# Four output buffers, other homes and places for some weight blocks, in a one-core encoder layer

## The reference

```python
proj = x @ w_in[i]
aq, ak, av, ag, bq, bk, bv, bg = jnp.split(proj, split_at, axis=-1)
ya = chunk_relbias_attention(aq, ak, av, rel_bias[i]) * jax.nn.silu(ag)
yb = sliding_window_sink_gqa(rope(bq), rope(bk), bv, sinks[i]) * jax.nn.silu(bg)
mix = jnp.concatenate([ya, yb], axis=-1) @ w_out[i]
h = DN_ALPHA * x + mix
h = h + jax.nn.sigmoid(h @ w_ple_gate[i]) * (p[i] @ w_ple_proj[i])
x = layer_norm(h, ln_g[i], ln_b[i])
```

## Time and profile before

| | us |
|---|---|
| median of 3 runs (2604.04 to 2610.0) | 2608.16 |
| the profiled execution, its own time | 2606.84 |
| its span, first to last instruction | 2605.1 |
| TensorE busy | 2480.7 (95%) |
| TensorE weight load busy | 2161.2 (83%) |
| VectorE busy | 1695.0 (65%) |
| ScalarE busy | 1193.5 (46%) |
| GpSimd busy | 379.3 (15%) |

### The profile page before, as it was taken

How to read it: one execution, slowest core, us unless ns; L and a number is a source line. 1 busy time by engine, 2 the same in 40 slices (tenths; PEclk the granted TensorE clock), 3 DMA queues, 4 the chain that set the end, 5 groups by cost and what they waited for, 6 DMA issues and landing times. The chain is left out here.

```text
span 2605.1 us, 37929 instructions
## 1 busy us (share of the span) xinstructions
PE 2480.7 (95%) x13620; PEld 2161.2 (83%) x13620; DVE 1695.0 (65%) x3215; ACT 1193.5 (46%) x2438; POOL 379.3 (15%) x226
## 2 busy tenths in 40 slices
PE   6999999999999999989999999968999999999997
PEld 4778887888789778989999998966888888888886
DVE  7887788768886888378888886863424333333333
ACT  4343443343333434278888887962222222222322
POOL 0100000000000000000000000123343434444341
PEclk9999999999999999999999998989999999999998
DMA  3645265435544554565666547965544545354540
GB/s 133 199 151 157 105 207 161 140 124 192 165 121 157 183 158 108 185 211 184 210 209 195 179 128 250 317 181 159 114 120 112 121 110 123 108 127 113 126 113 24
DMA packets 352693, 402.52 MB, mean 155 GB/s; under 512 B 83856, under 2 KB 257056, under 8 KB 346784
## 3 DMA queue, kind: packets, MB, share of 16 engines
q1 hardware_dynamic: 348544, 390.34, 50.8%
q0 software_dynamic: 4000, 10.25, 1.2%
HBM read 265.50 MB, written 136.07 MB: 154 GB/s over the span
## 5 line engine op out<-in xcount | busy, mean ns | idle before, releaser
L1638 DVE TENSOR_TENSOR y_lo<-y_raw,y_hi 128x1024 fp32r<-128x1024 f32 x32 | 39.2, 1226 | 396.2 <-ACT y_hi L1138 396.2
L980 ACT ACTIVATE wop_hi<-w_raw 128x512 fp32r<-128x512 f32 x288 | 174.1, 622 | 179.1 <-DVE w_raw L1279 153.6
L925 POOL DMA_DIRECT2D yb_d<-y_b x32 | 20.4, 637 | 1616.8 <-ACT y_b L1180 1591.0
L1538 DVE CUSTOM_DVE_ANT_0 prob<-psum,bias 128x640 f32<-128x640 f32 (+4 forms) x256 | 199.3, 778 | 73.6 <-issue 73.0
L1109 ACT ACTIVATE prob<-prob,small 128x640 f32<-128x640 f32 (+4 forms) x256 | 203.9, 797 | 60.7 <-DVE small L1538 60.7
L1740 PE MATMUL psum<-xs_lo_b,wop_hi 128*128 128x512 f32 x528 | 207.9, 394 | 0.0
L1740 PE MATMUL psum<-xt_hi,wop_hi 128*128 128x512 f32 x480 | 190.0, 396 | 16.7 <-issue 7.2
L1740 PE MATMUL psum<-wo_hi,y_hi 128*128 128x512 f32 x512 | 202.8, 396 | 1.3 <-DVE wo_lo L1633 1.3
L1554 DVE TENSOR_TENSOR pt_lo<-psum,pt_hi 128x640 fp32r<-128x640 f32 (+4 forms) x256 | 199.2, 778 | 4.2 <-ACT pt_hi L1118 4.2
L1740 PE MATMUL psum<-wo_hi,y_lo 128*128 128x512 f32 x512 | 200.2, 391 | 0.0
L1740 PE MATMUL psum<-wo_lo,y_hi 128*128 128x512 f32 x512 | 200.1, 391 | 0.0
(11 more groups left out here) (210 smaller groups left out, 6465.6 us busy)
## 6 DMA issues: line engine op xcount, KB each, us to landing
w_raw<-in_w_blocks SPq DMA_DIRECT2D x168, 256.0 KB, 3.9
qk_d<-stage_out SPq DMA_DIRECT2D x72, 512.0 KB, 4.1
v_d<-stage_out SPq DMA_DIRECT2D x64, 320.0 KB, 2.4
bq_d<-stage_out SPq DMA_DIRECT2D x64, 256.0 KB, 4.0
g_d<-stage_out SPq DMA_DIRECT2D x64, 256.0 KB, 2.3
ya_d<-y_a SPq DMA_DIRECT2D x128, 128.0 KB, 2.5
bq<-bq_d SPq DMA_DIRECT2D x32, 512.0 KB, 5.8
y_two<-ya_d SPq DMA_DIRECT2D x32, 512.0 KB, 4.6
```

Of the source, the lines that this page charges most:

```text
L925: pool.dma_start(yb_d[pair * P:pair * P + 4 * HEAD, t0:t0 + 4 * CHUNK].rearrange("(h d) t -> d h t", d=HEAD), y_b[:, d % 2, :, :]).then_in ...
L980: act.activation(wop_hi[:, n % W_RING, :, :], w_raw[:, i, :, :], ACT.Copy).then_inc(w_hi_done, 1)
L1538: dve.tensor_tensor_reduce(out=prob[:, r, NBW - n * P:NBW].rearrange("p (a b) -> p a b", a=2), in0=psum[:, 0:2, 0:n * P // 2], in1=bias[:, ...
L1638: dve.tensor_tensor(y_lo[:, :, :], y_raw[:, s, :, :], y_hi[:, :, :].bitcast(f32), ALU.subtract).then_inc(y_split, 1)
```

## The change

The product stage: A22 of the pairs 2, 4, 6 and 8 is loaded to a part of `x_raw_b`, that of the others to place 6 of `w_raw` as before (`a22(a)`), and from pair 2 on the load is issued with the other three blocks of its pair, at product (a-2, 6). At a group's change VectorE splits ring block 4 ahead of the low part of X22, and block 5 between it and the sums of T4. The attention of group B: `y_b` takes 128 partitions in place of 64, which gives four buffers, with four semaphores; a copy waits for the store of d-4. The passage: y tile 0 is split after strip 3 (step 67) in place of before strip 0 (step 64), on both engines; the reciprocals are copied before y tile 1 is split; w_ple's two strips get places of their own (`wp_raw`, over `wp_lo`) and are loaded right after strip 15. The matmuls, their order and the arithmetic are the same.

Context lines are left out of the diff.

```diff
@@ -58,8 +58,8 @@
-STRIP_SLOT = (0, 1, 2, 3, 4, 5, 11, 12, 3, 4, 5, 6, 7, 8, 9, 10, 6, 7)
-STRIPS = 13
+STRIP_SLOT = (0, 1, 2, 3, 4, 5, 11, 12, 3, 4, 5, 6, 7, 8, 9, 10, 13, 14)
+STRIPS = 15
@@ -285,6 +285,9 @@
+        def a22(a):
+            return x_raw_b[:, 1, 0, :].rearrange("p (k m) -> p k m", m=P) if a in (2, 4, 6, 8) else w_raw[:, 6, :, :]
+
@@ -315,7 +318,7 @@
-        y_b = sb("y_b", [HEAD, 2, 4, 4 * CHUNK])
+        y_b = sb("y_b", [P, 2, 4, 4 * CHUNK])
@@ -323,7 +326,9 @@
-        wp_hi, wp_lo = (sb(n, [P, 2, D_MODEL], f32r) for n in ("wp_hi", "wp_lo"))
+        wp_hi = sb("wp_hi", [P, 2, D_MODEL], f32r)
+        wp_raw = under("wp_raw", [P, 2, D_MODEL])
+        wp_lo = sb("wp_lo", [P, 2, D_MODEL], f32r)
@@ -351,7 +356,9 @@
-            return h[slot - 10][:, :]
+            if slot < 13:
+                return h[slot - 10][:, :]
+            return wp_raw[:, slot - 13, :]
@@ -396,7 +403,7 @@
-        by_stored = [sem(f"by_stored{i}") for i in range(2)]
+        by_stored = [sem(f"by_stored{i}") for i in range(4)]
@@ -491,6 +498,9 @@
+        def y_rows(d):
+            return slice(d % 4 // 2 * HEAD, d % 4 // 2 * HEAD + HEAD)
+
@@ -515,6 +525,12 @@
+                if b == 3 and a > 1:
+                    sp.wait_ge(x_split, 14 * (g + 1))
+                    if a > 2:
+                        sp.wait_ge(w_split, ring(g, a - 2, 6) + 1)
+                    sp.dma_start(a22(a), w_blocks[PAIRS[a][1] // P + 1, 1]).then_inc(w_loaded[3], 16)
+                    return
@@ -614,10 +630,10 @@
-                    if i == 2 and a + 1 < BK:
-                        load_w(g, a + 1, 3)
+                    if (a, i) == (0, 2):
+                        load_w(g, 1, 3)
...
-                        for b in range(3 if a < BK - 2 else 2):
+                        for b in range(4 if a < BK - 2 else 2):
@@ -813,7 +829,7 @@
-                        sp.wait_ge(stored, 16 * (3 * B_UNITS // 2))
+                        sp.wait_ge(stored, 16 * (3 * B_UNITS // 4))
@@ -829,8 +845,10 @@
-                sp.wait_ge(stored, 16 * (B_DOUBLES // 2))
+                sp.wait_ge(stored, 16 * (B_DOUBLES // 4))
...
+            for n in range(2 * KT, 2 * KT + 2):
+                load_strip(n)
@@ -839,10 +857,6 @@
-            for n in range(2 * KT, 2 * KT + 2):
-                sp.wait_ge(cw_split, n - 4)
-                load_strip(n)
-
@@ -923,7 +937,7 @@
-                             y_b[:, d % 2, :, :]).then_inc(by_stored[d % 2], 16)
+                             y_b[y_rows(d), d % 2, :, :]).then_inc(by_stored[d % 4], 16)
@@ -977,7 +991,7 @@
-                act.activation(wop_hi[:, n % W_RING, :, :], w_raw[:, i, :, :], ACT.Copy).then_inc(w_hi_done, 1)
+                act.activation(wop_hi[:, n % W_RING, :, :], a22(a) if i == 6 else w_raw[:, i, :, :], ACT.Copy).then_inc(w_hi_done, 1)
@@ -1175,9 +1189,9 @@
-                    if d >= 2:
-                        act.wait_ge(by_stored[d % 2], 16 * (d // 2))
-                    act.activation(y_b[:, d % 2, :, 0:2 * CHUNK].rearrange("p h (c q) -> p h c q", q=CHUNK),
+                    if d >= 4:
+                        act.wait_ge(by_stored[d % 4], 16 * (d // 4))
+                    act.activation(y_b[y_rows(d), d % 2, :, 0:2 * CHUNK].rearrange("p h (c q) -> p h c q", q=CHUNK),
@@ -1197,11 +1211,11 @@
-                if step == B_ALL:
+                if B_ALL <= step < B_ALL + KT:
+
+                    strip_hi(step - B_ALL)
+                if step == B_ALL + 3:
...
-                if B_ALL <= step < B_ALL + KT:
-
-                    strip_hi(step - B_ALL)
@@ -1225,8 +1239,8 @@
+            b_recip_copy(1)
...
-            b_recip_copy(1)
@@ -1258,14 +1272,14 @@
-                a11, a12, s2, a21, s3, s4, a22 = (w_raw[:, i, :, :] for i in range(7))
+                a11, a12, s2, a21, s3, s4 = (w_raw[:, i, :, :] for i in range(6))
...
-                    dst, x0, x1, how = a21, a21, a22, ALU.add
+                    dst, x0, x1, how = a21, a21, a22(a), ALU.add
@@ -1279,9 +1293,10 @@
-                _, _, i = ring_at(n)
+                _, a, i = ring_at(n)
+                raw = a22(a) if i == 6 else w_raw[:, i, :, :]
...
-                dve.tensor_tensor(wop_lo[:, n % W_RING, :, :], w_raw[:, i, :, :], wop_hi[:, n % W_RING, :, :].bitcast(f32),
+                dve.tensor_tensor(wop_lo[:, n % W_RING, :, :], raw, wop_hi[:, n % W_RING, :, :].bitcast(f32),
@@ -1456,7 +1471,7 @@
-                    for n in splits_at(g, s):
+                    for n in splits_at(g, s) if g == 0 or s > 0 else ():
@@ -1517,7 +1532,9 @@
+                    w_lo(72 * (g + 1) + 4)
...
+                    w_lo(72 * (g + 1) + 5)
@@ -1606,9 +1623,9 @@
-                    if d >= 2:
-                        dve.wait_ge(by_stored[d % 2], 16 * (d // 2))
-                    dve.tensor_copy(y_b[:, d % 2, :, 2 * CHUNK:4 * CHUNK].rearrange("p h (c q) -> p h c q", q=CHUNK),
+                    if d >= 4:
+                        dve.wait_ge(by_stored[d % 4], 16 * (d // 4))
+                    dve.tensor_copy(y_b[y_rows(d), d % 2, :, 2 * CHUNK:4 * CHUNK].rearrange("p h (c q) -> p h c q", q=CHUNK),
@@ -1640,10 +1657,10 @@
-                if step == B_ALL:
-                    y_tile_lo(0, 0)
...
+                if step == B_ALL + 3:
+                    y_tile_lo(0, 0)
```

More of the change, by code:

```diff
@@ L1199, in _ @@
                 b_step(step)
-                if step == B_ALL:
-                    y_tile_hi(0, 0, True)
                 if B_ALL <= step < B_ALL + KT:
                     strip_hi(step - B_ALL)
+                if step == B_ALL + 3:
+                    y_tile_hi(0, 0, True)
             def p_tile_hi(t, s, first=False):
```

## The result

The kernel after took **2570.83 us** (median of four runs, 2568.26 to 2572.91), the kernel before on the same chip 2606.78 (2604.04 to 2610.0). The medians are 36 us apart; the ratio is 0.9854, with a 95% interval of 0.9839 to 0.9870, which is 38 us less, 34 to 42. The forecast was 2563.5, its range 2551 to 2588. So direction and range held, and the time is 7 us above the forecast. The profiled execution after took 2569.48 us, with a span of 2567.7 against 2605.1 before: 37.4 us, where the sum had 44.7.

A forecast was written before the change was run, and what follows sets the result against it. TensorE, busy 2480.7 of 2605.1 us, was taken as the bound, leaving only its idle and clock dips. Product stage 25.0, `ple(0)` stall 17.8 and its dip 1.9 sum to 44.7: 2608.2 - 44.7 = 2563.5 us, range 2551 to 2588.

The forecast's parts named there:

- The term of 15.0: Product stage, two homes for A22: 15.0 of TensorE's 16.4 us of waits on `wop_lo` would go, 1.4 stay.
- the smaller of its own stall and VectorE's wait: Product stage: what TensorE gets back at each stall when VectorE's wait for the weight load goes; gave 15.0 us.
- The dips: Product stage: lowered TensorE clock behind stalls; three behind load stalls (5.1 us) and one at a group's change (1.6) would go.
- `vw_lo`'s 3.7 us: TensorE's waits on `vw_lo`, 3.7 us: not in the sum, counted as gone only in the best bounds (2551).
- 3.3 + 1.6 us: Group's change, weights split ahead of x: 1.1 us gained at each of three changes (3.3), one clock dip gone (1.6).
- the forecast's 25.0: Product stage in all: 15.0 load stalls, 5.1 clock dips behind them, 3.3 and 1.6 at the group's changes.
- the price of the ports: Passage: VectorE's strips beside GpSimd's tile 0 share SBUF ports, adding 4.1 us to VectorE's waits; last strip 10 us earlier.
- Rival 2: At `ple(0)`: 2.7 us of cover gone, strips 15 to 17 late; up to 7.8 us and a dip return, 2573; chance 0.15.
- y tile 2, x and p loads pay by 1 us of queue: Passage, w_ple strips loaded earlier: the loads behind them come 1 us later, covered by 12 us of gate and ple.
- Rival 1: Product stage: waits on stores replace those on loads, half the gain (12.5 us) returns, 2576; chance 0.14.
- Rival 4: SP: 32 moved loads hold up stores, so the kernel gets slower; 2618 at 1.7 us per load; chance 0.04.
- Rival 3: Passage: buffers don't help, VectorE's queue order and GpSimd's tile 0 set the 10.55 us stall; 2580 to 2586; chance 0.05.

## Why the prediction was right, and where its sizes were off

**Two homes.** Right in mechanism and place: 45.3 us of VectorE's waits became 0.7, in the kernel after no dip of the clock was left in the stage past 120 us (five before; with this edit alone two, one of them behind a new stall of 2.86), and this edit alone gave 22.4 us at the start of attention. The term of 15.0 was too large. `wop_lo` fell from 16.4 to 5.1 without the three waits at a group's change: 11.3. The step that failed is "the smaller of its own stall and VectorE's wait". It holds where nothing but the load was late. With the load out of the way something else ended last just behind it (read from the traces, not tried by itself). Of the 3.7 us too much, 1.9 are the three waits behind VectorE's unbroken queue (its own work, at 393 us for instance), and 1.8 the waits in the four gate pairs, where it is ScalarE and the store it waits for. At 692.20 us before, TensorE's 2.07 had a load wait of 2.01 ahead and so counted in full; after, 0.69 of it is left. The dips were undersized in turn: five of 1.5 to 1.7 us stood in the trace before, 8.3 in all, where the forecast took 6.7. Likewise `vw_lo`'s 3.7 us, which the prediction held back for its lower end, are gone.

**Group's change.** The local working was right: 1.16, 1.16 and 1.17 us where it said 1.2. But the forecast's 3.3 + 1.6 us for it are wrong as a gain of the program. Alone and undone on top, it changes nothing that is measured. The step that failed is that a stall shortened at one product is a gain at the stage's end. At the next stall it counts where VectorE is and not where TensorE could be, and VectorE has the same work in another order: at 400 us it was 1.1 later on the kernel before and 0.5 earlier on the kernel after. What takes the rest of the gain by the stage's end was not traced. By count from the two traces the stage's gain is 11.3 + 3.7 at the changes + 3.7 `vw_lo` + 8.3 dips = 27.0, near the measured 27.5. That this is also near the forecast's 25.0 is partly luck: one term was too large (the homes' stalls), one is worth nothing by itself (the order), two were too small (dips, `vw_lo`). And kernels that share the code of this stage start attention anywhere between 1080.7 and 1087.2 us.

**Four buffers and tile 0.** Right in mechanism, 7.3 us where the forecast had 10. The step that failed is the price of the ports. One strip waited for two GpSimd operations in a row: 3.7 us, and 1.6 for the next, 5.3 in all against 4.1. Of the other 1.5 us missing, 1.2 lie ahead of the strips: the copy of double 28 ends 30.2 us behind the reciprocals' first transpose, where the forecast had 29.1. Why was not traced. On the Trainium skill's rule (page "SBUF — State Buffer", section "SBUF: two separate sides") that VectorE and GpSimd take the shared pair in turns, the trace agrees: 4.90 and 2.77 us for strips that take 1.2 alone. It does not agree with the page's "starts first gets the pair for the whole instruction": the strip whose record starts first was held for the whole of two operations that start after it.

**ple(0).** 16.8 us from the reciprocals' transpose, where the forecast had 17.8 over the same stretch. The sum came so close by luck: the 2.7 us missing at the strip were partly made up by `mix(1)`, which took 11.0 us where the forecast kept the 12.8 of the kernel before, with the dip of the clock behind its 3.63 us stall. With the strips late again 8.6 come back, the stall of the earlier trace rows (7.79) and a little. Rival 2, the cover gone, did not happen: no wait on `p_lo` is left.

**What was not in the sum: y tile 2.** This is the step that failed in the last stage: "y tile 2, x and p loads pay by 1 us of queue, with 12 us of gate and ple in front of them". Tile 2's data had that cover. GpSimd's wait for `lng` and `lnb` did not. Both are issued after tile 2's loads, in a quiet queue before and right behind a full one after (DMA share before 0.04 from 1782 to 1786 us; after, 1.14 from 1732 to 1736 and 0.61 from 1736 to 1740):

| | issued | GpSimd starts | us |
|---|---|---|---|
| before | 1784.89 | 1790.70 | 5.8 |
| after | 1740.04 | 1750.70 | 10.7 |
| after, w_ple's strips late again | 1756.16 | 1762.25 | 6.1 |

That left a stall of 5.21 us where 1.19 was: 4.0 us, and the transposes behind it ran at a lower clock, 1.96 us for eight where 1.09 is usual. The run with the wait moved shows it: the stall, its dip and 5.4 us of the passage go, and the last stage's steady part (second transposes to last `ple`) is 777.3 us, as before (777.4), where the kernel after has 779.8. All fourteen traces fall in these two classes: 777.3 to 778.5 us in the seven whose stall on `h` is at most 1.6, 779.7 to 780.5 in the seven where it is 3.4 or more. With this one line the gain is 48.3 us (2612.79 less 2564.52), and the forecast had 44.7; but the kernel before was slower there than in the forecast, and the kernel with only the reciprocals' copy undone, run beside it, gained 42.8. So the line itself is worth some 5 us there and 7.7 where it was tried with the earlier tile 0.

**Rivals.** Rival 1 (stores take the place of the loads, 12.5 us) fell as a whole: ScalarE's waits for stores to free a slot came to 86.7 us before and 79.0 after. It is right in the four gate pairs above, where it has 1.8 us of the 3.7. VectorE's waits for ScalarE at the values and at the gate pairs were 47.7 and 16.5 us before; after:

```profile
DVE stage_out L1398 <- ACT stage_out L1050: 41.8, 64, 2.7
...
DVE stage_out L1382 <- ACT stage_out L1038: 19.4, 16, 2.6
```

Rival 4 (SP) fell with it, for the same 86.7 and 79.0. Rival 3 (the buffers don't do it) fell: with two buffers the stall of 5.2 us on the store returns. Its point on GpSimd's tile 0 was half right: with the buffers alone the second stall grows to 11.61.

**A loss in attention.** From the start of attention A to the reciprocals' transpose 2.3 us of the product stage's 27.5 were lost again: 1.3 in attention A, which no edit touches, and 1.0 in B. Attention A took 469.5 to 470.9 us over all fourteen traces, so its part is spread. What is known of B stands in the last section.

## What to carry to other kernels

A stall is only worth what the releasers behind it have spare: before a reorder is priced, look at the next products, at what the engine that is waited for waits for there and whether it idles at all. If the next load, store or full queue is as late, the time comes back at the next wait. Where one wait of an engine goes, look at the waits just ahead of it too: the next longest can take its place. When loads are moved earlier, list every wait in the program that is on a load issued after them in the same queue, also those for small, unrelated tensors. They get later, and a wait that had 1 us to spare in an empty queue can stop TensorE. After a move, look for the next wait of the chain (here `ple(0)`, then `h`) and not only for the one removed.

## What the runs showed of the hardware

**A copy to the other half of the partitions.** With four buffers in 128 partitions, two of four copies of `y_b` go from PSUM's first 64 partitions to partitions 64 to 127. VectorE after, such a copy between its neighbours:

```profile
1692.96 0.69 DVE L1622 TENSOR_REDUCE small<-psum 128x4 f32<-128x512 f32 x1
1693.68 0.68 DVE L1628 COPY y_b<-psum 64x512 f32<-64x512 f32 x1
1694.39 0.23 DVE L1636 TENSOR_SCALAR b_shift<-small,sink_sb 128x4 f32<-128x4 f32 x1
```

The copy starts 0.72 us after the reduce and the next 0.71 after the copy. Before, the same two distances are 0.61 and 0.60:

```profile
1700.54 0.69 DVE L1605 TENSOR_REDUCE small<-psum 128x4 f32<-128x512 f32 x1
1701.15 0.67 DVE L1611 COPY y_b<-psum 64x512 f32<-64x512 f32 x1
1701.75 0.21 DVE L1619 TENSOR_SCALAR b_shift<-small,sink_sb 128x4 f32<-128x4 f32 x1
```

So an instruction whose output starts in another half waits out its predecessor's end, and so does the one after it, 0.11 us each. The Trainium skill (page "VectorE: DVE Perf Modes", section "Two Vector instructions with no wait between them") calls such an instruction held, by the quadrant in which its output starts; the trace agrees. Attention B up to the reciprocals took 112.1 to 115.4 us in four runs with two buffers and 112.7 to 116.4 in ten with four. The means are 1.7 apart but the ranges overlap. The two-buffer kernel's 112.7 is 3.7 less than in the first trace of the kernel after (116.4), which is how it gets back most of its longer passage; but the kernel after once more, with four buffers, took 112.7 too. So that gain needs no cause beyond the spread, and a cost of the held copies to the whole run is possible but not shown. It was not tried apart from the buffers.

**The port pair.** One VectorE instruction, a strip of 4.90 us where 1.2 is usual, was held by two GpSimd operations in a row (1.28 and 2.34 us), and its record starts 0.24 us ahead of the first.

**A dip of the clock can move.** With tile 0 earlier, the dip at `mix(0)` went and one came at `mix(1)` (the clocks above). When a stall of some 2 us is followed by a dip stayed open: the three stalls of 2.4 us at the group's changes had two dips behind them in the kernel before (the first and third), two with the four buffers alone (the first and second), and one with the two homes alone (the first) and with the order undone on the kernel after (the second). So the dips of this stage, five in the kernel before, are not a fixed number: with four buffers alone and the same product stage there were three.
